# Where the squares of a norm are summed: VectorE adds or TensorE one-column matmuls, in a two-layer trunk

## The reference

```
def rmsnorm(x, g):
    xf = x.astype(F32)
    y = xf * lax.rsqrt(jnp.mean(xf * xf, axis=-1, keepdims=True) + EPS)
    return (y * g.astype(F32)).astype(x.dtype)
...
def trunk_layer(x, mod, lw, lam, l_init, ffn, ctx):
    shift1, scale1, gate1, shift2, scale2, gate2 = jnp.split(mod, 6, axis=-1)
    h = rmsnorm(x, lw['norm_mix']) * (1 + scale1) + shift1
    y, state = token_mixer(h, lw, lam, l_init, ctx)
    x = x + gate1 * y
    h = rmsnorm(x, lw['norm_ffn']) * (1 + scale2) + shift2
    x = x + gate2 * ffn(h)
    return x, state
```

## Time and profile before

| | |
|---|---|
| median of three runs | 2245.5 us |
| all runs | 2251.76, 2245.5, 2242.22 us |
| the profiled execution's own time | 2251.76 us |
| its span in the trace | 2249.9 us |
| mean granted clock of TensorE | 0.92 of full speed |
| PE busy | 1977.0 us (88%) |
| DVE busy | 1464.5 us (65%) |
| ACT busy | 1077.2 us (48%) |
| POOL busy | 306.9 us (14%) |

### The profile page before, as it was taken

How to read it: one execution, slowest core, us unless ns; L and a number is a source line. 1 busy time by engine, 2 the same in 40 slices (tenths; PEclk the granted TensorE clock), 3 DMA queues, 4 the chain that set the end, 5 groups by cost and what they waited for, 6 DMA issues and landing times.

```text
span 2249.9 us, 28772 instructions
## 1 busy us (share of the span) xinstructions
PE 1977.0 (88%) x11347; PEld 1762.9 (78%) x11347; DVE 1464.5 (65%) x1995; ACT 1077.2 (48%) x1427; POOL 306.9 (14%) x433
## 2 busy tenths in 40 slices
PE   6899578988899999997987679897499999999994
PEld 2699467778899999997986567796378888888883
DVE  6755767443666666645476675434278888888887
ACT  6524466642321121123234566523367777777772
POOL 0025631000011111000074420000100000000001
PEclk8899689979899999998998799897699999999997
DMA  9412000011455455432221000000789999999996
GB/s 385 152 59 93 21 1 1 1 57 59 132 171 183 147 179 190 150 94 61 62 72 43 1 1 1 1 1 1 290 307 389 394 399 396 397 397 392 392 383 227
DMA packets 115912, 375.67 MB, mean 167 GB/s; under 512 B 8640, under 2 KB 66400, under 8 KB 89408
## 3 DMA queue, kind: packets, MB, share of 16 engines
q1 hardware_dynamic: 94448, 303.50, 35.9%
q0 software_dynamic: 14240, 51.49, 6.8%
q10 hardware_dynamic: 7088, 18.81, 2.2%
HBM read 347.13 MB, written 26.64 MB: 166 GB/s over the span
## 4 chain that ended last, share of the span: by engine, by line
PE 73%; DVE 14%; ACT 7%; issue 3%; DMA 2%; POOL 1%; SPq 0%; ACTq 0%; DVEq 0%; POOLq 0%
PE PS L1888 30%; PE PS L1829 24%; PE PS L1868 5%; PE PS L1589 5%; PE PS L1695 4%; DVE NM L1097 2%; ACT E L767 2%; PE PS L1669 2%; DVE SS L1467 1%; DVE NT__178 L1364 1%; DMA araw<-in_w_ada_head 1%; DMA rows_of_slots<-HTM,SLI 1%; ACT PT L774 1%; PE PS L1917 1%; PE PS L1750 1%
## 5 line engine op out<-in xcount | busy, mean ns | idle before, releaser
L1888 PE MATMUL PS<-H,split 128*128 128x320 f32 x2688 | 402.0, 312 | 13.2 <-DVE H L1523 11.1
L1888 PEld LDWEIGHTS PS<-H,split 128*128 128x128 f32 x2688 | 400.9, 191 | 14.2 <-issue 14.2
L942 ACT CAST split<-raw 128x2048 fp32r<-128x2048 f32 (+2 forms) x64 | 112.8, 1762 | 265.2 <-PE PS L1888 229.3
L1331 DVE TENSOR_TENSOR split<-raw,split 128x2048 fp32r<-128x2048 f32 (+2 forms) x64 | 138.0, 2161 | 131.3 <-ACT split L942 131.1
L1249 DVE TENSOR_TENSOR split<-raw,split 128x2048 fp32r<-128x2048 f32 x82 | 186.9, 2290 | 51.4 <-ACT split L895 51.4
L1249 DVE TENSOR_TENSOR msplit<-raw,msplit 128x2048 fp32r<-128x2048 f32 x82 | 187.9, 2292 | 32.2 <-ACT msplit L895 32.1
L1829 PE MATMUL PS<-split,HT 128*128 128x512 f32 x816 | 198.7, 400 | 5.4 <-DVE HT L1228 5.4
L1097 DVE TENSOR_REDUCE NM<-PS 128x1 f32<-128x640 f32 (+1 forms) x180 | 123.6, 714 | 104.8 <-PE PS L1669 104.5
L1829 PE MATMUL PS<-msplit,HT 128*128 128x512 f32 x816 | 190.5, 389 | 0.0
L895 ACT CAST msplit<-raw 128x2048 fp32r<-128x2048 f32 x82 | 156.9, 1914 | 64.1 <-PE PS L1829 64.1
L895 ACT CAST split<-raw 128x2048 fp32r<-128x2048 f32 x82 | 157.2, 1917 | 61.1 <-PE PS L1829 46.3
(11 more groups left out here) (300 smaller groups left out, 3082.0 us busy)
## 6 DMA issues: line engine op xcount, KB each, us to landing
raw<-in_moe_w_gate SPq DMA_DIRECT2D x55, 1024.0 KB, 7.2
raw<-in_moe_w_down SPq DMA_DIRECT2D x55, 1024.0 KB, 7.8
raw<-in_moe_w_up SPq DMA_DIRECT2D x54, 1024.0 KB, 7.0
DOTW<-in_w_ada_rows POOLq DMA_DIRECT2D x56, 512.0 KB, 4.4
mraw<-in_moe_w_up SPq DMA_DIRECT2D x14, 1024.0 KB, 7.8
mraw<-in_moe_w_gate SPq DMA_DIRECT2D x13, 1024.0 KB, 7.0
mraw<-in_moe_w_down SPq DMA_DIRECT2D x13, 1024.0 KB, 7.5
raw<-in_w_ada_head SPq DMA_DIRECT2D x12, 1024.0 KB, 14.9
```

The lines of the kernel that those rows point to most:

```text
L942: A.copy(split[u % 2][:, 0, 0:w], src[:, 0:w]).then_inc(S["split_hi"], 1)
L1331: V.tensor_tensor(split[u % 2][:, 1, 0:w], src[:, 0:w], split[u % 2][:, 0, 0:w].bitcast(f32), ALU.subtract).then_inc(S["split_lo"], 1)
L1888: ins = T.matmul(PS[:, 4 * (u % 2) + 2 * c + hf, 0:HALF], W[:, w, k, c * P:(c + 1) * P], A[:, a, k, hf * HALF:(hf + 1) * HALF], start=(k = ...
```

## The change

VectorE's adds of squares are removed, and with them the tile `XACC` and the semaphore `x_summed`. Instead TensorE takes each chunk of squares as weights as soon as ScalarE has made it (`x_sums(q, kc)`), five one-column matmuls for each chunk, each into its own PSUM column, and counts `sq_used`. For q = 0 the 40 columns lie in bank 0; for the others in banks 0, 2, 4 and 6, ten in each, beside the columns of the products. VectorE then reduces 40 columns to 5 (a `tensor_reduce` into `XTMP`) and makes the mean from them. In the modulation stage `x_sums` stands at `j` = 9 to 16, and `x_mean(0)` moves behind the loop. In the output projections and the down projection the sums of chunks 2j-2 and 2j-1 stand behind the product of unit j, and those of the last two chunks behind the last product's.

```
-        XACC = at("XACC", [P, TOK], OFF_U)
...
-        XSUM = PS[:, 0, HALF:HALF + NT]
+        XSUM = PS[:, 0:8:2, HALF:HALF + 2 * NT].rearrange("p b (k t) -> p b k t", t=NT)
+        XSUM0 = PS[:, 0, HALF:HALF + KC * NT].rearrange("p (k t) -> p k t", k=KC)
...
-            def x_acc(q, kc):
-
-                if kc == 0:
-                    return
-                dve.wait_ge(S["sq_ready"], q * KC + kc + 1)
-                if kc > 1:
-                    dve.wait_ge(S["sq_used"], q * KC + kc)
-                acc = XACC[:, :] if q else XSQ[:, 0, :]
-                first = (HM[:, 0, :] if q else XSQ[:, 0, :]) if kc == 1 else acc
-                V.tensor_tensor(acc, first, HM[:, kc % 2, :] if q else XSQ[:, kc, :], ALU.add).then_inc(
-                    S["sq_used"], 2 if kc == 1 else 1)
-
             def x_mean(q):
-                dve.wait_ge(S["x_summed"], q + 1)
-                V.tensor_scalar(XMEAN[:, :], XSUM, 1.0 / D_MODEL, EPS, ALU.mult, ALU.add).then_inc(S["x_mean"], 1)
+                dve.wait_ge(S["sq_used"], (q + 1) * KC)
+                if q:
+                    ch.then(V.tensor_reduce(XTMP[:, :], XSUM.rearrange("p b k t -> p t b k"), op=ALU.add, axis=AX.XY))
+                else:
+                    ch.then(V.tensor_reduce(XTMP[:, :], XSUM0.rearrange("p k t -> p t k"), op=ALU.add, axis=AX.X))
+                V.tensor_scalar(XMEAN[:, :], XTMP[:, :], 1.0 / D_MODEL, EPS, ALU.mult, ALU.add).then_inc(S["x_mean"], 1)
...
-                if SUM_UNIT <= j < SUM_UNIT + KC:
-                    x_acc(0, j - SUM_UNIT)
-                if j == SUM_UNIT + KC + 1:
-                    x_mean(0)
+            x_mean(0)
             modulation_out(ADA_BLOCKS - 3)
...
                 product(u, KC, MIX)
+                if j:
+                    for c in range(2):
+                        x_sums(2 * l + 1, 2 * j - 2 + c)
...
                     product(u, KC if k < 2 * pairs else kd, H if k < 2 * pairs else ACTB, r, ready)
+                    if last and k > 2 * pairs:
+                        for c in range(2):
+                            x_sums(2 * l + 2, 2 * (k - 2 * pairs) - 2 + c)
...
-            def x_sum(q):
-                pe.wait_ge(S["sq_used"], (q + 1) * KC)
+            def x_sums(q, kc):
+                pe.wait_ge(S["sq_ready"], q * KC + kc + 1)
                 for t in range(NT):
-                    squares = XACC[:, t * P:(t + 1) * P] if q else XSQ[:, 0, t * P:(t + 1) * P]
-                    ins = T.matmul(XSUM[:, t:t + 1], squares, ones[:, 0:1], start=True, stop=True)
-                ins.then_inc(S["x_summed"], 1)
+                    squares = HM[:, kc % 2, t * P:(t + 1) * P] if q else XSQ[:, kc, t * P:(t + 1) * P]
+                    ins = T.matmul(XSUM[:, kc % 4, kc // 4, t:t + 1] if q else XSUM0[:, kc, t:t + 1], squares, ones[:, 0:1],
+                                   start=True, stop=True)
+                ins.then_inc(S["sq_used"], 1)
...
-                if j == SUM_UNIT + KC:
-                    x_sum(0)
+                if SUM_UNIT <= j < SUM_UNIT + KC:
+                    x_sums(0, j - SUM_UNIT)
...
                     if q:
-                        x_sum(q)
+                        for kc in range(KC - 2, KC):
+                            x_sums(q, kc)
                         x_rows(q)
```

More of the change, by code:

```diff
@@ L1273, in moe_dve, with ffn_dve, round_ @@
                     V.tensor_tensor(XTM[:, t, :], XTM[:, t, :], y, ALU.add).then_inc(S[done], 1)
-        def ffn_dve(V, dve, ch, l, base, split_lo, gated_add, dots, x_acc):
+        def ffn_dve(V, dve, ch, l, base, split_lo, gated_add, dots):
             rounds, tail = layer_rounds(l)
             acts0 = 0 if l == 0 else 4 * DENSE_ROUNDS + TAIL_PAIRS
-            def round_(r, u0, pairs, extra, ahead, last=False):
+            def round_(r, u0, pairs, extra, ahead):
                 d_pairs, d_u = extra
@@ L1300, in round_ @@
                         split_lo(u0 + k + 2, r)
-                    if last and k > 2 * pairs:
-                        for c in range(2):
-                            x_acc(2 * l + 2, 2 * (k - 2 * pairs) - 2 + c)
                     n = 2 * (u0 + k - base - U_FFN)
@@ L1310, in ffn_dve @@
                 round_(None, u0 + r * ROUND, 4, (r * 4, 0), True)
-            round_(None, u0 + rounds * ROUND, tail, (rounds * 4, 0), True, last=True)
+            round_(None, u0 + rounds * ROUND, tail, (rounds * 4, 0), True)
         @block.vector
@@ L1497, in _ @@
                     if q:
-                        for kc in range(KC - 2, KC):
-                            x_acc(q, kc)
                         x_mean(q)
@@ L1558, in _, with mixer_pe @@
                                 split_lo(u + 2)
-                            if j:
-                                for c in range(2):
-                                    x_acc(2 * l + 1, 2 * j - 2 + c)
                     elif l == 0:
-                        ffn_dve(V, dve, ch, l, base, split_lo, gated_add, dots, x_acc)
+                        ffn_dve(V, dve, ch, l, base, split_lo, gated_add, dots)
                     else:
                         moe_dve(V, dve, ch)
-        def mixer_pe(T, pe, l, base, turn, product, h_ready):
+        def mixer_pe(T, pe, l, base, turn, product, h_ready, x_sums):
             for j in range(3):
@@ L1839, in moe_pe, with ffn_pe, round_ @@
                 piece(n)
-        def ffn_pe(T, pe, l, base, turn, product, h_ready):
+        def ffn_pe(T, pe, l, base, turn, product, h_ready, x_sums):
             rounds, tail = layer_rounds(l)
             acts0 = 0
-            def round_(r, u0, pairs, kd, d_pairs):
+            def round_(r, u0, pairs, kd, d_pairs, last=False):
                 def act_ready(k):
@@ L1860, in ffn_pe @@
                 round_(r, u0, 4, KC, r * 4)
-            round_(None, u0 + rounds * ROUND, tail, TAIL_FF // P, rounds * 4)
+            round_(None, u0 + rounds * ROUND, tail, TAIL_FF // P, rounds * 4, last=True)
         @block.tensor
```

6 lines of the change are left out of this document (3 added, 3 removed).

## The result

The median of 14 executions is 2260.84 us (2246.17 to 2278.27), beside 2247.23 us (2233.3 to 2256.32) of the kernel before, 14 executions as well. The ratio is 1.0076, with a 95% interval from 1.0053 to 1.0098: 17 us slower, where 19 were forecast. Measured again beside the last experiments it was 1.0047 (1.0025 to 1.0068), which is 11 us (6 to 15).

The account below looks back on a forecast made before the run. It took TensorE, with 73% of the chain of waits, as the bound. Modulation stage +4.5, first two boundaries +10.4 and third +4.4 summed to +19.3 us, giving a forecast of 2264 us, range 2249 to 2281.

Parts of the forecast that it names:

- the results of units 2 and 3: Sign in the out projection: these results come 16.5 us apart or more, against 14.08 before.
- The price of a group: Five one-column matmuls between products cost 1.19 us at the upper clock level; four groups add 4.8 us per boundary.
- The gain behind the last product: From last product to mean, 1.3 us saved at each of the first two norm boundaries, 2.1 at the third.
- groups 6 and 7: Last two chunks' sums, behind the last product: they wait for ScalarE's squares and at the lower level end at 564.8.
- The 3.5 us for the upper level: Gain behind the last product at the first boundary if the clock stayed at its upper level: mean at 563.15.
- Clock spells at the boundaries: One fall to the lower clock among the paired groups ahead of each boundary's last product, +1.7 us each.
- The modulation stage without spells: TensorE's queue from 48.9 us to the first norm's broadcast takes 34.3 us, ending at 83.2 instead of 82.04: +1.1.
- The modulation stage with spells: Two more spells at the lower clock level in the modulation stage, +3.4 us, making +4.5 there.
- rival 5: Modulation stage at the lower clock nearly throughout, +20 us or more there, total above 2280; chance 0.06.
- Rival 3: Clock kept at the boundary by TensorE's work on groups 4 to 7: not slower, -1.3 us, 2244; chance 0.08.

Follow-up runs that it names:

- after_2: The changed kernel run again, unaltered, against the kernel before: median 2260.28 us, ratio 1.0047.
- wide: The changed kernel with 128 columns of ones instead of one in every column sum (norms wrong): median 2250.44 us, ratio 1.0008 to the kernel before.
- q0_only: The kernel before with the change in the modulation stage alone: median 2251.88 us, ratio 1.0004; repeated, 2244.22 us, 0.9993.
- singles: The changed kernel with groups of chunks 0 to 3 set singly inside products, not in pairs between them: median 2264.22 us, ratio 1.0074 to the kernel before.
- bounds_only: The changed kernel with the modulation stage of the kernel before: median 2248.25 us, ratio 0.9993 to the kernel before; repeated, 2251.4 us, 1.0002.
- early: The kernel before with chunks 0 to 5 added earlier, three sum groups behind the product, table load and squares before cast, weight split behind root: 2231.05 us, ratio 0.9924.

## Why the prediction was right, and where it was right by luck

The total holds (+17 and +11 measured, +19.3 in the sum), its direction too, and the mechanism of its rows is in the traces. Its parts hold less well: from 47 us to the first broadcast and at the boundaries the three traces of the changed kernel are 24.4 to 25.0 us longer, where 19.3 were forecast, and 7 to 11 us come back in stages without a term. That the total came out near the forecast is thus partly luck. Of the signs named beforehand, the results of units 2 and 3 were to be 16.5 us apart or more; they are 17.85 and 16.30, and in the later traces 16.30 and 16.31, since most products had no fall.

- **The price of a group.** Taken: 1.19 us. Measured: 2.22 us for two between products (16.30 - 14.08), and for two behind a unit of the down projection. 4.4 us per boundary instead of 4.8.
- **The gain behind the last product.** Taken: 1.3, 1.3 and 2.1 us. Measured to the mean 1.44, 1.43 and 3.37, to the broadcast 1.42, 1.43 and 2.91; in after_2, to the broadcast, 1.43, 2.17 and 1.32. At the first two boundaries the waits of groups 6 and 7, the low level and the reduce (0.20 us taken and measured) came as worked out. At the third the moment of the fall was taken from the first boundary, 4 us behind the product; it came at 4.7 us in one trace and at 2.0 in two, and the forecast 2.1 lies between what they gained. The 3.5 us for the upper level came out too: wide gains 3.4.
- **Clock spells at the boundaries.** Taken: one of 1.7 us at each. Measured: 1.5 us each, but only six in the 30 places of five traces (three boundaries with two products each), two in the changed kernel's first trace and one in each of the next. +10.7, +10.0 and +10.1 us for the three boundaries instead of 14.8.
- **The modulation stage without spells.** Taken: 34.3 us of PE queue, +1.1. Measured: broadcasts at 82.9 to 83.4 in three traces (q0_only twice, singles), even with one spell in them. The units were sized a little short: without any fall (wide) PE's queue takes 35.5 us from 48.99 to the broadcast, not 34.3. But the fair comparison is with the same course of the clock up to 47 us: 79.2 to 80.8 in the six traces with the old stage and a short early spell, so +3.3. The kernel before had its 82.04 with the later course.
- **The modulation stage with spells.** This term was the wrong size. Taken: +3.4 for two spells. In all three traces of the changed kernel the clock fell four times up to 90 us, each time for about seven microseconds with about three between, and 10.3 us more were lost than before: +14.3 (14.6 and 14.3 in the other two traces) instead of +4.5. It is a milder form of rival 5, which had a chance of 0.06.
- **What the sum had no term for.** Clock spells in unchanged stages come and go, between programs and between traces of one. In the profiled execution they lost 9.3 us less before the experts; in the two later traces not, but there each of the two stretches from a norm's broadcast through the mixer behind it is 2.9 to 3.2 us shorter. Over all executions the sum divides thus: "upper" +12.5 us (+13.7 the second time), where 1.1 + 14.4 - 4.7 = 10.8 was forecast; "lost" +2.6 (-2.3 the second time, each with a standard error of about 2), where 8.5 was forecast. The forecast's gains of 4.7 are times at the clock of their stage, so the two divisions match only roughly. The larger loss in the modulation stage and the savings elsewhere offset each other in part; my smaller loss, with nothing given back, came out near the same place.
- **Rival 3**, the clock kept, was partly true: not at the boundary, as I had it, but elsewhere, and only in bounds_only does it make the kernel not slower (9 to 13 us less "lost", against 10 to 12 more "upper"). What it would be at the boundary is seen in wide: +1.1 us to the broadcast, where its first two terms, 4.8 - 3.5, make 1.3.

"Upper" is about additive: 3.1 or 4.2 us for the one half and 12.3 or 10.2 for the other, 12.5 or 13.7 for both. "Lost" is not: -2.8 or -5.7 and -13.0 or -8.9, but +2.6 or -2.3 for both, with standard errors of 2 to 3 us each.

Open are: why only the changed kernel has the repeated falls while q0_only and singles have not; what sets the course of the clock up to 47 us and in the stages that were not changed; and whether single groups are safer at a boundary than pairs.

## What to carry to other kernels

Moving small sums from a free VectorE into a bound TensorE costs each group its weight loads, 1.1 us for five float32 matmuls here, between products and inside them alike; only behind the last product, where PE waited anyway, did groups cost nothing or gain. Look first at what the square itself waits for, since the order on ScalarE and VectorE (table load, square, cast; adds ahead, weight split behind) was worth 10 of the 15 us that early gained in the traces. If small matmuls must stand in a dense stream, price them with the granted clock beside them, and try more moving columns before taking them out. Where edits each measure as nothing but together as something, split each execution's time into span x clock and span x (1 - clock): the first adds up better, and the second says how much the clock may be; then look in the traces at which stages it moved.

## What the hardware showed that I had not expected

- 128 moving columns instead of one in the same 160 matmuls (320 records) made "upper" 7 us more and "lost" 22 us less (6 and 17 beside after_2). A busy TensorE alone did not hold the clock: in the changed kernel it fell to 0.50 with PE busy for 2.00 of 2.00 us, at 52 to 56 and again at 64. The Trainium skill ("TensorE: Matmul & The Clock Gate", Part 1) has the upper rate for a busy engine. The rows at 52 to 56 differ from it, if busy is what the trace calls busy; wide's rows agree.
- Executions of one kernel spread by 32 us in span (2244.3 to 2276.4, 36 executions), and most of it goes with the clock: the spans have a standard deviation of 7.9 us, span x clock one of 2.1. The Trainium skill ("TensorE: Matmul & The Clock Gate", HAM oscillation) reckons a throttled stretch as costing half its length, and "lost" counts that half. These executions come near it: each microsecond so counted went with 0.82 us of span.
- Five one-column matmuls with weights of their own cost as much inside a product of 320-column matmuls as between two: 1.15 us from the first of their ten loads to the product's next in singles. The Trainium skill ("TensorE: Matmul & The Clock Gate", Engine queue depths) says that PE can pull weight loads ahead of matmuls in flight. The rows agree for the product's own loads, 36 in 5.29 us beside 36 matmuls; for a group they leave room for one load in ten at most.
- A reduce of 128x40 to 128x5 that reads four banks of PSUM took 0.20 us, no more than one from a single tile.
